# Head square sums by a block matrix of ones, with the inverse roots taken per channel

## The reference

```python
# retention: the values are centred beforehand, so the mean is already gone
o = head_layernorm(o_f + flip(o_b))            # (o - mu) * rsqrt(var + 1e-6) over 64 channels
o_ret = o * silu(g)
# differential attention
o_diff = rmsnorm(o_diff, g_diff) * (1 - lam_init)   # o * rsqrt(mean(o*o) + 1e-6) * gain, over 64 channels
```

## Time and profile before

| | |
|---|---|
| median of 3 runs | 2319.7 us (2318.75 to 2321.82) |
| the profiled execution | 2321.85 us, span in the profile 2319.70 us |
| PE busy | 2287.5 us, 99% of the span |
| DVE busy | 1275.7 us, 55% |
| ACT busy | 924.5 us, 40% |
| POOL busy | 750.1 us, 32% |
| granted TensorE clock, mean | 0.996 of full speed |

### The profile page before, as it was taken

One profiled execution on the slowest core, in us unless ns is written; L12 is line 12 of the kernel. 1 busy time (PEld: TensorE's weight loads), 2 busy tenths in 40 slices (PEclk: granted clock), 3 DMA queues, 4 the chain that ended last, 5 costly groups with the idle time before them and its releaser, 6 DMA issues.

```text
span 2319.7 us, 40593 instructions
## 1 busy us (share of the span) xinstructions
PE 2287.5 (99%) x17116; PEld 2062.1 (89%) x17116; DVE 1275.7 (55%) x2234; ACT 924.5 (40%) x1763; POOL 750.1 (32%) x498
## 2 busy tenths in 40 slices
PE   7999999999999999999999999999999999999998
PEld 5888898888989998998988879888889899899897
DVE  4436458644336763763664373685444467547556
ACT  3335346634335331331362452555442443223223
POOL 0331221211433544544422303121123435544442
PEclk9999999999999999999999999999999999999999
DMA  9413222223242324223232142222232322222211
GB/s 317 139 57 121 76 95 81 78 74 107 100 127 73 91 91 128 73 91 123 78 137 75 39 134 92 85 67 92 74 110 84 108 91 74 76 70 78 87 60 68
DMA packets 221906, 221.62 MB, mean 96 GB/s; under 512 B 10582, under 2 KB 191390, under 8 KB 221470
## 3 DMA queue, kind: packets, MB, share of 16 engines
q1 hardware_dynamic: 212999, 193.77, 26.2%
q10 hardware_dynamic: 8727, 25.27, 3.2%
HBM read 209.90 MB, written 9.11 MB: 94 GB/s over the span
## 4 chain that ended last, share of the span: by engine, by line
PE 93%; DVE 3%; ACT 3%; issue 1%; POOL 1%; DMA 0%; SPq 0%; POOLq 0%; DVEq 0%; ACTq 0%
PE ps L896 50%; PE ps L1027 12%; PE ps L1564 11%; PE ps L1486 4%; PE ps L1168 3%; PE ps L1185 2%; PE ps L916 2%; PE ps L1129 1%; PE ps L1144 1%; PE ps L992 1%; PE ps L1114 1%; PE ps L1388 1%; PE ps L1150 1%; PE ps L907 1%; POOL w_lo L855 1%
## 5 line engine op out<-in xcount | busy, mean ns | idle before, releaser
L855 POOL TENSOR_TENSOR w_lo<-raw,w_hi 128x512 fp32r<-128x512 f32 (+1 forms) x486 | 739.9, 1552 | 1547.6 <-ACT w_hi L1636 992.8
L896 PE MATMUL ps<-h_hi,w_hi 128*128 128x320 f32 (+2 forms) x2368 | 615.2, 312 | 0.0
L896 PE MATMUL ps<-h_hi,w_lo 128*128 128x320 f32 (+2 forms) x2368 | 607.2, 309 | 0.0
L896 PE MATMUL ps<-h_lo,w_hi 128*128 128x320 f32 (+2 forms) x2368 | 606.6, 309 | 0.0
L896 PEld LDWEIGHTS ps<-h_hi,w_hi 128*128 128x128 f32 x2368 | 413.4, 188 | 7.1 <-issue 4.6
L896 PEld LDWEIGHTS ps<-h_lo,w_hi 128*128 128x128 f32 x2368 | 413.4, 188 | 0.2
L896 PEld LDWEIGHTS ps<-h_hi,w_lo 128*128 128x128 f32 x2368 | 412.9, 188 | 0.0
L1636 ACT ACTIVATE w_hi<-raw 128x2048 fp32r<-128x2048 f32 (+2 forms) x110 | 203.7, 1852 | 268.7 <-PE ps L1564 95.0
L2650 DVE TENSOR_SCALAR conv<-u_pad,vcol 128x642 f32<-128x642 f32 x88 | 90.1, 1023 | 151.1 <-ACT u_pad L2072 149.5
L1564 PE MATMUL ps<-w_hi,a_hi 128*128 128x512 f32 x440 | 172.3, 392 | 0.6 <-POOL w_lo L855 0.6
L1564 PE MATMUL ps<-w_lo,a_hi 128*128 128x512 f32 x440 | 171.3, 389 | 0.0
(11 more groups left out here) (348 smaller groups left out, 3475.8 us busy)
## 6 DMA issues: line engine op xcount, KB each, us to landing
raw<-in_w_mod SPq DMA_DIRECT2D x44, 1024.0 KB, 5.1
raw<-in_w_up SPq DMA_DIRECT2D x88, 512.0 KB, 4.8
raw<-in_w_gate SPq DMA_DIRECT2D x32, 1024.0 KB, 5.4
raw<-in_w_in SPq DMA_DIRECT2D x16, 1024.0 KB, 5.1
raw<-in_w_down SPq DMA_DIRECT2D x16, 1024.0 KB, 5.0
w_br<-in_w_branch ACTq DMA_DIRECT2D x8, 1024.0 KB, 5.0
raw<-in_w_out SPq DMA_DIRECT2D x8, 1024.0 KB, 5.6
raw<-in_w_down SPq DMA_DIRECT2D x8, 768.0 KB, 4.4
```

The lines of the kernel that those rows point to most:

```text
L855: ins = nc.gpsimd.tensor_tensor(w_lo[part_slot(li, s)][:, c0:c1], raw[HOME[u]][:, c0:c1], w_hi[part_slot(li, s)][:, c0:c1].bitcast(F32), A ...
L896: ins = mm(out, w_at(w_hl[wi]), at_(x_hl[xi]), start=first and q == 0, stop=final and q == 2)
```

## The change

The sums of squares are formed with the operands the other way round. The weights are now `blocks`, a constant 128 by 128 matrix with ones in the two diagonal 64 by 64 blocks and zeros elsewhere, and the squares are streamed: one product of 512 columns and one of 128 per channel tile. Each output row (channel) then holds the sum of its own head, so sums, roots and inverses have the shape 128 channels by 640 tokens. The widening copy and the ten transposes per norm disappear, as do their waits. ScalarE takes the root over 640 columns per tile, and VectorE takes the reciprocal over 640 columns per tile, in place, before the product that uses it. In the differential norm the two `head_sums` stand between the second and the third `uq` product, ScalarE takes their roots between the second and the third `z_mq`, and VectorE's reciprocals stand after its `rope`, in front of line 2586's products. In the retention norm the two `head_sums` are parts 0 and 1 of `ret_norm`, and the second waits for the first root since both use bank 5.

```diff
-            V.memset(ones[:], 1.0).then_inc(made.sem, 1)
+            for p0 in (0, 64):
+                V.memset(blocks[p0:p0 + 64, p0:p0 + 64], 1.0).then_inc(made.sem, 1)
+                V.memset(blocks[p0:p0 + 64, 64 - p0:128 - p0], 0.0).then_inc(made.sem, 1)
...
-                def head_sums(sq_, b):
-
-                    for c2 in range(2):
-                        for t in range(T):
-                            c0 = 2 * (T * c2 + t)
-                            last = mm(bank(b, c0, c0 + 2), sq_[:, c2, t * P:(t + 1) * P], c("side"), start=True, stop=True)
-                    return last
-
-                def turn_rstd(rec, c2, b):
-
-                    for t in range(T):
-                        last = tr(bank(b, t * P, t * P + P), rec[:, T * c2 + t].rearrange("p j d -> p (j d)"), ident)
-                    return last
+                def head_sums(sq_, c2, b):
+
+                    mm(bank(b), blocks[:], sq_[:, c2, 0:BANK], start=True, stop=True)
+                    return mm(bank(b + 1, 0, P), blocks[:], sq_[:, c2, BANK:TOK], start=True, stop=True)
...
                 def ret_norm(part):
 
+                    if part == 2:
+                        return
                     if part == 0:
                         pe.wait_ge(ro_done.sem, now(ro_done, T))
                         pe.wait_ge(rg_done.sem, now(rg_done, T))
-                        head_sums(ret_sq, 5).then_inc(rv_mm.sem, 1)
                     else:
-                        pe.wait_ge(rx_done.sem, now(rx_done, 1))
-                        if part == 2:
-                            pe.wait_ge(rx_read.sem, now(rx_read, 1))
-                        turn_rstd(ret_rec, part - 1, 5).then_inc(rx_mm.sem, 1)
+                        pe.wait_ge(rv_act.sem, now(rv_act, 1))
+                    head_sums(ret_sq, part, 5).then_inc(rv_mm.sem, 1)
...
-                head_sums(o_sq, slot()).then_inc(mla_mm.sem, 1)
                 w = raw_unit("uq")
                 for t in range(T):
+                    for c2 in range(2 if t == 2 else 0):
+                        head_sums(o_sq, c2, slot()).then_inc(mla_mm.sem, 1)
...
-                pe.wait_ge(ox_done.sem, now(ox_done, 1))
-                for c2 in range(2):
-                    turn_rstd(o_rec, c2, slot()).then_inc(mla_mm.sem, 1)
...
-                ret_root()
+                ret_root(0)
                 round_unit()
-                take_z(2)
+                take_z(2, (0,))
+                ret_root(1)
+                take_z(2, range(1, T))
...
-                sc.wait_ge(mla_mm.sem, now(mla_mm, k + 1))
-                act_(st5[:, 2, :], bank(mla_bank(k), 0, 4 * T), ACT.Sqrt, bias=eps_c[:], scale=1.0 / 64).then_inc(mla_done.sem, 1)
-                k += 1
                 for t in range(T):
+                    for c2 in range(2 if t == 2 else 0):
+                        sc.wait_ge(mla_mm.sem, now(mla_mm, k + 1))
+                        act_(o_rms[:, c2, :], bank(mla_bank(k), 0, TOK), ACT.Sqrt, bias=eps_c[:], scale=1.0 / 64).then_inc(mla_done.sem, 1)
+                        k += 1
                     take(z_mq[:, t, :], P, 384)
                 for q in range(2, 4):
                     round_quarter(q)
-                for c2 in range(2):
-                    take(o_rms[:, c2, :], P, TOK)
...
-                ve.wait_ge(rv_act.sem, now(rv_act, 1))
-                widen(ret_rec).then_inc(rx_done.sem, 1)
                 for c2 in range(2):
-                    ve.wait_ge(rx_mm.sem, now(rx_mm, c2 + 1))
-                    tt(ret_g[:, c2, :], ret_g[:, c2, :], bank(5, 0, TOK), ALU.mult).then_inc(rx_read.sem, 1)
+                    ve.wait_ge(rv_act.sem, now(rv_act, c2 + 1))
+                    V.reciprocal(ret_rms[:, c2, :], ret_rms[:, c2, :]).then_inc(vstep.sem, 1)
+                    ve.wait_ge(vstep.sem, step())
+                    tt(ret_g[:, c2, :], ret_g[:, c2, :], ret_rms[:, c2, :], ALU.mult).then_inc(rx_read.sem, 1)
...
-                ve.wait_ge(mla_done.sem, now(mla_done, 5))
-                widen(o_rec).then_inc(ox_done.sem, 1)
...
                 for c2 in range(2):
-                    ve.wait_ge(mla_done.sem, now(mla_done, 5 + T + c2 + 1))
+                    ve.wait_ge(mla_done.sem, now(mla_done, 6 + c2 + 1))
+                    V.reciprocal(o_rms[:, c2, :], o_rms[:, c2, :]).then_inc(vstep.sem, 1)
+                    ve.wait_ge(vstep.sem, step())
                     stt(o_t[0][:, c2, :], o_t[0][:, c2, :], vcol[:, GDIFF:GDIFF + 1], o_rms[:, c2, :], ALU.mult, ALU.mult).then_inc(diff_o.sem, 1)
```

More of the change, by code:

```diff
@@ L79 @@
 MLP = mlp_order()
-CONST_COLS = dict(ident=P, side=2, fold=4, colf=1, colb=1, mprev=P, mnext=P, dpos=P, upf=P, dneg=P, upb=P, rowf=P, rowb=P,
+CONST_COLS = dict(ident=P, pad=2, fold=4, colf=1, colb=1, mprev=P, mnext=P, dpos=P, upf=P, dneg=P, upb=P, rowf=P, rowb=P,
                   c16=NL * 64, s16=NL * 64, c8=NL * 32, s8=NL * 32)
@@ L104, in shape_constants @@
     put("fold", i[:, None] % 32 == np.arange(4))
-    put("side", i[:, None] // 64 == np.arange(2))
     put("mprev", np.where(col >= row, 0.0, NEG))
@@ L343, in build @@
         const = at("const", [P, n_const])
-        ones = at("ones", [P, P])
+        blocks = at("blocks", [P, P])
         vcol = at("vcol", [P, 317])
@@ L390, in build @@
         ret_sq = at("ret_sq", [P, 2, TOK], offset=OR)
-        ret_rec = at("ret_rec", [P, 2 * T, 2, 64], offset=OR)
-        o_rec = at("o_rec", [P, 2 * T, 2, 64], offset=Z0 + 5120)
+        ret_rms = at("ret_rms", [P, 2, TOK], offset=OR)
         ret_g = at("ret_g", [P, 2, TOK], offset=PTR)
@@ L543, in build @@
         rg_mm, rg_act, rg_done = Signal("ret_gate_turned", T), Signal("ret_gate_tanh", T), Signal("ret_gate_ready", T)
-        rv_mm, rv_act, rx_done, rx_mm = Signal("ret_square_sums"), Signal("ret_rms"), Signal("ret_rstd_widened"), Signal("ret_rstd_turned", 2)
-        rx_read, ox_done = Signal("ret_rstd_used", 2), Signal("diff_rstd_widened")
+        rv_mm, rv_act, rx_read = Signal("ret_square_sums", 2), Signal("ret_rms", 2), Signal("ret_rms_used", 2)
         ret_o, diff_o = Signal("ret_normed", 2), Signal("diff_normed", 2)
@@ L553, in build @@
         prep_in, prep_act, prep_done = Signal("mla_sums", 2), Signal("mla_by_scalar", 4), Signal("mla_normed")
-        MLA_ITEMS = 4 + 1 + T + 2 + 2 + (T + 1) + 4
+        MLA_ITEMS = 4 + 2 + T + 2 + (T + 1) + 4
         mla_mm, mla_done = Signal("mla_product", MLA_ITEMS), Signal("mla_ready", MLA_ITEMS)
@@ L732, in raw_released @@
                 return [(mod_mm, counts(li)(mod_mm, MOD_ORDER.index(i) + 1))]
-            return [(mla_mm, counts(li)(mla_mm, {"uq": 5 + T, "ukv": 7 + T + 2 + T + 1}[kind]))]
+            return [(mla_mm, counts(li)(mla_mm, {"uq": 6 + T, "ukv": 6 + T + 2 + T + 1}[kind]))]
         def parts_released(s):
@@ L871, in _ @@
             pe.wait_ge(cond_done.sem, 2)
-            pe.wait_ge(made.sem, 4)
+            pe.wait_ge(made.sem, 7)
             for li in range(DEPTH):
@@ L1291, in _ @@
                     if r == 0:
-                        pe.wait_ge(rx_read.sem, now(rx_read, 2))
+                        pe.wait_ge(rv_act.sem, now(rv_act, 2))
                     b = (4, 0, 2)[r]
@@ L1610, in _ @@
             act_(stat[:, 0:2, :].rearrange("p a b -> p (a b)"), cond[:], ACT.Sigmoid).then_inc(cond_sig.sem, 1)
-            sc.wait_ge(made.sem, 4)
+            sc.wait_ge(made.sem, 7)
             act_(stat[:, 6, 0:1], eps_c[:], ACT.Sqrt)
@@ L1766, in take_ret_gate, with ret_root @@
                     act_(ret_g[:, :, t * P:(t + 1) * P], bank(6, 0, BW).rearrange("p (k n) -> p k n", k=2), ACT.Tanh, scale=0.5).then_inc(rg_act.sem, 1)
-                def ret_root():
-                    sc.wait_ge(rv_mm.sem, now(rv_mm, 1))
-                    act_(st5[:, 2, :], bank(5, 0, 4 * T), ACT.Sqrt, bias=eps_c[:], scale=1.0 / 64).then_inc(rv_act.sem, 1)
+                def ret_root(c2):
+                    sc.wait_ge(rv_mm.sem, now(rv_mm, c2 + 1))
+                    act_(ret_rms[:, c2, :], bank(5, 0, TOK), ACT.Sqrt, bias=eps_c[:], scale=1.0 / 64).then_inc(rv_act.sem, 1)
                 def take_heads(br, t):
@@ L2110, in _ @@
             V.memset(cond_c[:], 0.0).then_inc(made.sem, 1)
-            ve.wait_ge(made.sem, 4)
+            ve.wait_ge(made.sem, 7)
             ve.wait_ge(cond_t.sem, 1)
@@ L2511, in _ @@
                         ALU.add, ALU.mult).then_inc(rg_done.sem, 1)
[L2514 to L2518, removed]
                 flat = lambda ap: ap.rearrange("p k n -> p (k n)")
@@ L2578, in _ @@
                 ins.then_inc(w2_high.sem, 1)
-                ve.wait_ge(mla_done.sem, now(mla_done, 5))
-                widen(o_rec).then_inc(ox_done.sem, 1)
                 rope(z_mq[:, 1:T, 256:384].rearrange("p t (h c) -> p t h c", h=4), 4, 8, c("c8"), c("s8"), rope_tmp[3][:],
-                     lambda t: ve.wait_ge(mla_done.sem, now(mla_done, 5 + t + 1)))\
+                     lambda t: ve.wait_ge(mla_done.sem, now(mla_done, 4 + 2 * (t > 1) + t + 1)))\
```

(4 more changed lines are left out.)

## The result

The changed kernel takes 2349.26 us (median of 4 runs, 2346.70 to 2349.91) against 2319.77 before (4 runs): a ratio of 1.012, 95% interval 1.0108 to 1.0133. That is 29.5 us slower, where 12.8 us slower was forecast, and above the top of the range.

The account below looks back on a forecast made before the run. PE was taken to bound the kernel, busy 2287.5 of 2319.7 us. Per layer 1.0 + 3.0 + 2.4 = 6.4, twice +12.8 us, gave 2334.6 profiled and a forecast median of 2332.5 us (+0.55%), range 2325 to 2341.

Parts of the forecast that it names:

- The reciprocal's 4.1 us: On VectorE, each 640-column reciprocal was to take 4.1 us, from the slope of small ones; bounds 3.8 and 4.4.
- Eight passes: Rival: on VectorE a reciprocal costs eight passes, 5.5 us each, giving 2343.7 us; chance 0.04.
- streaming: Rival: on VectorE a 640-element reciprocal costs about what a product does, 0.8 us, giving 2312.7 us; chance 0.08.
- The differential norm: PE waits 5.3 us for `diff_o` at `attention(3)`, starting 3.0 us later per layer; half clock behind it costs 2.4.
- The 2.3 us by which PE comes to its end earlier: In the differential norm PE reaches the key products 2.3 us early: 1.2 from the transposes, the rest from the clock.
- The full clock among the `uq` products: In the differential norm, the half clock from 438.90 to 442.20 was expected to go with wide products instead of two-column ones.
- Queued behind is `rope`: four blocks of 1.85 us: In the retention norm, `rope` follows the reciprocals and products on VectorE, taking 7.4 us and ending at 173.2.
- +1.0: In the retention norm, PE waits for `rope_done` and starts 1.0 us later per layer; bounds +0.4 and +2.0.
- Behind the retention wait of 2.1 us I take no drop: After PE's 2.1 us wait for `rope_done`, the clock was to stay up, at no cost.
- The rival of a second drop: Rival: the clock drops after the retention wait too, 1.6 to 2.4 us more per layer, 2336 to 2337 us; chance 0.16.

Follow-up runs that it names:

- the hold on GpSimd: The changed kernel with GpSimd's subtraction for the low part of gate unit (0, 3) held until `rope` is done: 2336.61 us, ratio 1.0063.

## Why the prediction was wrong

- **The reciprocal's 4.1 us** was right (4.15), and with it the sign: the slope over sizes of 5 to 20 held at 640. Eight passes and streaming are both out.
- **The differential norm** came out right: 2.67 us where 3.0 stood, and 2.63 for the clock where 2.4 stood. The 2.3 us by which PE comes to its end earlier are there (453.92 - 442.92 = 11.00 us, 448.00 - 434.66 = 13.34 before). On VectorE two smaller misses cancel, which is luck: `rope`'s last product met GpSimd here as well (its group ran from 455.63 to 460.64) and took 1.32 us instead of 0.29, and the two products with the gain took 0.89 us each, with GpSimd at rest, where 1.6 and 1.0 to 1.6 stood.

```profile
455.74 1.32 DVE L2296 TENSOR_TENSOR z_mq<-z_mq,rope 128x128 f32<-128x128 f32 x1
...
466.14 0.89 DVE L2568 SCALAR_TENSOR_TENSOR o_t<-o_t,vcol,o_rms 128x640 f32<-128x640 f32 x1
```

- **The full clock among the `uq` products** came as forecast in the changed kernel. As a gain it is less certain than it looked, since the two-column sums are not always followed by a half clock.
- **The failed step is the retention norm's "Queued behind is `rope`: four blocks of 1.85 us", and its +1.0.** The blocks cost 1.85 us where the earlier trace rows show them, and were moved some 4 us later without a look at what runs there. GpSimd's subtractions do: its row of before, 171.44 to 178.41, lies directly behind `rope`, and `o_lo`'s 2.45 us beside it was the warning. The prediction spoke of products that stretch while GpSimd works, but as 1.1 us that become 1.6. Small ones fared worse: three of 0.25 us became 1.31 to 1.35. In place of +1.0 the shift was 5.90. Without this overlap PE waits 2.78 us, 4.18 less, and the shift would be 5.90 - 4.18 = 1.7, inside the bounds of +0.4 to +2.0; most of the 0.7 that is left is GpSimd again, the product with `o_t` that took 1.80 us where 1.1 stood (and that 1.1 itself ran beside GpSimd; without it the product takes 0.82).
- **"Behind the retention wait of 2.1 us I take no drop"** held in the one traced wait near that size at this place (the hold on GpSimd: 2.78 us, no drop) and fell with the wait's size: behind 6.96 us the clock was at half and cost 2.1. It was less safe than it looked, since a drop did follow the 2.32 us in the run without reciprocals. The rival of a second drop gave 1.6 to 2.4, but at a wait of 2.1, and so 2336 to 2337.

By terms, per layer: forecast 1.0 + 0 + 3.0 + 2.4 = 6.4, measured 5.90 + 2.10 + 2.67 + 2.63 = 13.30. The missing 6.9 us lie in the retention norm, and 4.18 + 2.10 = 6.3 of them came back when the one overlap was taken out.

On the overlap itself the trace comes first. The third block's first small product starts at 170.36, ahead of GpSimd, and takes 0.25 us. The other three take 1.31 to 1.35 us each, and each ends 0.11 to 0.12 us after a GpSimd subtraction does (171.88 after 171.76, 173.11 after 173.00, 174.35 after 174.23). The subtractions take 1.27 to 1.29 us each, no longer than with VectorE at rest (1.30 and 1.28 in the kernel before, from 175.88 on). Single instructions of VectorE and GpSimd:

```profile
170.53 1.35 DVE L2290 TENSOR_TENSOR rope<-z,const 128x96 f32<-128x96 f32 x1
...
171.72 1.28 POOL L852 TENSOR_TENSOR w_lo<-raw,w_hi 128x512 fp32r<-128x512 f32 x1
171.80 1.31 DVE L2290 TENSOR_TENSOR rope<-z,const 128x96 f32<-128x96 f32 x1
```

So each small product waits for one whole subtraction, while the one long product that makes `o_lo` waits for one in all (1.49 us in the changed kernel, where GpSimd rests, 2.45 beside GpSimd in the kernel before). The Trainium skill, SBUF — State Buffer, section "Who interferes with whom", says so: a VectorE instruction with both inputs in SBUF contends with a GpSimd instruction that reads SBUF, the one that issues first holds the shared ports for its whole length, and the other is blocked. The rows of the single instructions agree with it.

## What to carry to other kernels

An operation that is hidden may be made longer only up to what is left before the engine that sets the end arrives, and every instruction queued behind it moves too: look up what the other engines do at the place where it will land, above all GpSimd against small VectorE products with two SBUF inputs. Widening a statistic so that a matrix product can replicate it multiplies each later step on it: here the reciprocal went from 20 to 640 elements per partition at 6.2 ns each, and a form that saved PE 1.2 us of transposes per norm cost VectorE 8.3. When PE must wait several us, count the half clock behind the wait as well, 2.1 to 2.6 us here.

## What the runs showed of the hardware

A reciprocal's cost on VectorE is linear from 20 to 640 elements, 6.2 ns per element beside 1.3 for a product. A VectorE product of 0.25 us with two inputs in SBUF that started beside a GpSimd subtraction of 1.28 us took 1.31 to 1.35. PE's clock was at half behind waits of 4.95 and 6.96 us and, in one run, of 2.32; it stayed up behind 0.81, 1.01 and 2.78; spare products in place of the wait keep it up. Whether two-column products are followed by a half clock differs between the traces, and what decides it isn't shown: in the kernel before it came after the differential norm's sums only, with the differential norm alone changed it came after the retention norm's, and with the retention norm alone changed not after the sums that were left. ScalarE went from Ln to Exp and back with a 1.28 us table load each time.
